# Placing attention's background steps by the vector and scalar work of each slot

## What is computed

```python
h = x @ w_in                                  # q | k | v | u, 512 columns each
z = q k^T / 8;  mask: key before query        # 8 heads of 64
log_beta = log_sigmoid(z); log_1m = where(mask, log_beta - z, 0)
after = reverse_cumsum(log_1m) - log_1m
a_out = where(mask, exp(log_beta + after), 0) @ v      # stick-breaking attention
p_out = ((trailing mean of u, windows 2,4,8,16) - u) @ pool_w * pool_scale
x1 = LayerNorm(ALPHA*x + concat[a_out, p_out] @ w_out)
y  = LayerNorm(ALPHA*x1 + (silu(x1 @ w_gate) * (x1 @ w_up)) @ w_down)
```

## Time and profile before

| | us |
|---|---|
| runs | 2577.51, 2580.75, 2580.77 (median 2580.75) |
| the profiled execution's own time | 2577.73 |
| its span (first to last instruction) | 2576.0 |
| TensorE busy | 2513.8 |
| VectorE busy | 1571.3 |
| ScalarE busy | 1153.8 |
| GpSimd busy | 1173.1 |
| granted TensorE clock, share of full speed | 0.998 |

### The profile page before, as it was taken

The page is one execution under the profiler, slowest core; times in us unless marked ns, Lnnn a source line. Parts: engine busy times, 40 slices in busy tenths (PEclk is TensorE's granted clock), DMA queues, the critical chain, the costliest instruction groups (busy, mean ns, idle before and its releaser), DMA issues.

```text
span 2576.0 us, 37571 instructions
## 1 busy us (share of the span) xinstructions
PE 2513.8 (98%) x13882; PEld 2143.7 (83%) x13882; DVE 1571.3 (61%) x2125; ACT 1153.8 (45%) x1932; POOL 1173.1 (46%) x1028
## 2 busy tenths in 40 slices
PE   9999999999999999999999999999999999999998
PEld 9978788788878878878788887878878887899997
DVE  3266247676444366787734567887775355866776
ACT  4466326664323135666532265656554213433333
POOL 4465437754323145565532174556653214354434
PEclk9999999999999999999999999999999999999999
DMA  7698946773456233444263244343533522323232
GB/s 232 201 275 258 365 159 197 236 218 116 130 155 216 82 107 112 126 123 119 80 227 131 90 115 119 103 112 110 155 91 114 203 66 92 97 91 115 94 95 84
DMA packets 210134, 374.30 MB, mean 145 GB/s; under 512 B 29760, under 2 KB 104128, under 8 KB 207904
## 3 DMA queue, kind: packets, MB, share of 16 engines
q1 hardware_dynamic: 209952, 371.89, 45.8%
HBM read 303.73 MB, written 68.09 MB: 144 GB/s over the span
## 4 chain that ended last, share of the span: by engine, by line
PE 81%; DVE 6%; issue 3%; POOL 3%; DMA 3%; ACT 2%; SPq 1%; DVEq 0%; POOLq 0%; ACTq 0%
PE bank L1315 26%; PE bank L1377 19%; PE bank L1265 8%; PE bank L1219 7%; PE bank L1323 7%; PE bank L1116 5%; PE bank L1164 4%; PE bank L1132 4%; DMA gw_lo_raw<-in_w_in_dram 1%; DVE left L1947 1%; POOL gw_lo L2617 1%; DVE acc L1985 1%; PE bank L1242 1%; POOL later_lad L2643 1%; DVE stats L1967 0%
## 5 line engine op out<-in xcount | busy, mean ns | idle before, releaser
L1315 PE MATMUL bank<-x1T,gw_hi 128*128 128x512 f32 (+1 forms) x2336 | 712.9, 389 | 3.7 <-DVE hT_lo_raw L2061 2.3
L2547 POOL TENSOR_TENSOR beta<-beta,left 128x512 f32<-128x512 f32 (+2 forms) x326 | 353.0, 1083 | 348.0 <-DVE left L1947 347.4
L1315 PEld LDWEIGHTS bank<-x1T,gw_hi 128*128 128x128 f32 x2336 | 419.0, 189 | 83.7 <-issue 3.2
L1315 PE MATMUL bank<-x1T,gw_lo 128*128 128x512 f32 (+1 forms) x1168 | 448.1, 384 | 0.0
L2574 POOL TENSOR_TENSOR gw_lo<-gw_lo_raw,gw_hi 128x1024 fp32r<-128x1024 f32 x70 | 181.8, 2597 | 423.1 <-ACT gw_hi L1569 422.9
L1492 ACT ACTIVATE aT<-bank 128x512 fp32r<-128x512 f32 (+2 forms) x326 | 173.6, 533 | 426.1 <-PE bank L1132 377.0
L1265 PE MATMUL bank<-x1T,gw_hi 128*128 128x256 f32 (+2 forms) x1472 | 353.4, 332 | 3.2 <-POOL gw_lo L2617 1.3
L2242 DVE TENSOR_TENSOR acc<-bank,acc 128x512 f32<-128x512 f32 x312 | 213.4, 686 | 211.0 <-PE bank L1377 207.6
L1932 DVE TENSOR_TENSOR aT<-bank,aT 128x512 fp32r<-128x512 f32 (+2 forms) x326 | 197.0, 604 | 195.1 <-ACT aT L1492 193.7
L1377 PE MATMUL bank<-dw_hi,hT_hi 128*128 128x512 f32 x728 | 295.2, 405 | 9.8 <-issue 5.8
L1377 PE MATMUL bank<-dw_lo,hT_hi 128*128 128x512 f32 x728 | 286.6, 394 | 0.0
(11 more groups left out here) (223 smaller groups left out, 4697.8 us busy)
## 6 DMA issues: line engine op xcount, KB each, us to landing
gw_lo_raw<-in_w_gate_dram SPq DMA_DIRECT2D x88, 512.0 KB, 3.6
gw_lo_raw<-in_w_up_dram SPq DMA_DIRECT2D x88, 512.0 KB, 3.7
dw_lo_raw<-in_w_down_dram SPq DMA_DIRECT2D x86, 512.0 KB, 4.4
gw_lo_raw<-in_w_in_dram SPq DMA_DIRECT2D x64, 512.0 KB, 4.4
k_st<-kT_scratch SPq DMA_DIRECT2D x160, 128.0 KB, 4.1
v_st<-v_scratch SPq DMA_DIRECT2D x80, 256.0 KB, 4.3
q_st<-qT_scratch SPq DMA_DIRECT2D x128, 128.0 KB, 4.0
wo_raw<-in_w_out_dram SPq DMA_DIRECT2D x16, 1024.0 KB, 5.6
```

Source lines behind the costliest of these rows:

```text
L1315: m = pe.matmul(gu_bank(g, n)[:, 0:w], gw[L % 4][a][:, k, :], x1T[x][:, k, first:first + w], start=k == 0 and s == 0, stop=k == KD - 1 and ...
L2547: pool.tensor_tensor(x[:, 0:w], x[:, 0:w], left[n % RL][:, 1:w + 1], ALU.mult).then_inc(a_done, 1)
```

## The change

A new function `level` moves attention's steps after `spread` has placed them. `slots_work` holds for every slot an amount of foreground work of VectorE and of ScalarE, and `step_work` gives what one step adds to each, and to TensorE. `level` walks through the slots with a backlog for both engines that shrinks by 2 a slot (and by the step's own TensorE amount), and places the next step in the first slot, at most EARLY = 3 before its even one, where the backlog is not over a limit; if a step came LATE = 5 or more after its even slot, the limit is raised by 0.1 and the block is done again. At most one step stands in a slot, as before. The steps of the other 32 tokens are not moved by the work.

Worked through by its own numbers, this moves 40 of 44 steps in block 0, 51 of 82 in block 1, 103 of 108 in block 2 and 133 of 140 in block 3; 14, 10, 76 and 104 of them by the full three slots earlier. First steps stay where they were. Neighbouring slots now hold steps more often: the longest unbroken row of steps has 12 slots in block 0 (before 4) and 8 in the others (before 3, 2 and 2). Slots 512 to 519 and 776 to 783 (down products and turned tokens between two blocks) held five steps each and hold none now.

On SyncE, block 0's residual tokens are loaded at m = 12 to 15 and its norm rows at m = MIX_ADD + 2*4 = 25 (the others' stay at 13), and `load_px` stands at slots 30, 33, 36, 39. In block 0's mixing (slots 131 to 188) that puts the residual tokens at slots 150 to 155 (before 139 to 153), the norm rows at 171 (before 152) and the next tokens at 158 to 167 (before 144 to 150). Nothing else of the program changes.

```diff
--- before.py
+++ after.py
@@ -627,12 +627,121 @@
             due.setdefault(first + before * (end - first) // total, []).append(tick)
             before += w
 
+    slots_work = [[0.0, 0.0] for _ in range(FP + SLOTS * BLOCKS)]
+
+    def add_work(s, vector, scalar):
+        if s < len(slots_work):
+            slots_work[s][0] += vector
+            slots_work[s][1] += scalar
+
+    for n in range(NP):
+        b, kind, c = place(n)
+        S = done_slot(n)
+        if n % 16 == 14 and b < BLOCKS - 1:
+            add_work(S, 1.8, 0)
+        if n + 3 < NP:
+            add_work(next(s for s, x in split_at.items() if x == n + 3), 0, 1.5)
+        if kind in (KEY, QUERY):
+            add_work(S, 1, 1.7 if kind == KEY else 0.85)
+        elif kind == VALUE:
+            add_work(S, 0, 0.85)
+            add_work(S + 4, 1, 0.85)
+        else:
+            add_work(S, 0, 0.85)
+            add_work(S + c + 1, 1, 0)
+            add_work(S + 5, 2, 0.85)
+            add_work(S + 8, 1.1, 1)
+    for b in range(1, BLOCKS):
+        for s in (-4, -3, 0, 1):
+            add_work(PS * b + s, 1.8, 1.5)
+    for s in (-4, -2, 0, 2):
+        add_work(FP + s, 1.9, 1.9)
+    for b, s in KC_AT:
+        add_work(PS * b + s + 1, 1, 0.85)
+
+    at_slot = FP
+    for b in range(BLOCKS):
+        for p in range(PAIRS):
+            for group in range(4):
+                if group == 1 and p:
+                    for _ in range(2 * tiles_of(b)):
+                        add_work(at_slot, 1, 0)
+                        at_slot += 1
+                for i in range(4):
+                    if group == 0 and p:
+                        add_work(at_slot, (1, 0, 1.2, 0)[i], (0, 0.85, 0, 0)[i])
+                    add_work(at_slot, ((0, 0, 0, 2.1), (0, 1, 0, 0), (1, 2.1, 1.2, 0), (0, 1, 0, 0))[group][i],
+                             ((0, 0, 1.5, 0), (0.85, 0, 1.5, 0), (1.5, 0.85, 0, 1.5), (0.85, 1.5, 0, 1.5))[group][i])
+                    if b and (p, group, i) in ((0, 0, 1), (0, 0, 2), (0, 0, 3), (1, 0, 0)):
+                        add_work(at_slot, 2.2, 0)
+                    if b and (p, group, i) in ((1, 1, 1), (1, 1, 2), (1, 1, 3), (2, 0, 0)):
+                        add_work(at_slot, 2.5, 0)
+                    at_slot += 1
+        if b < BLOCKS - 1:
+            for d in range(2 * BT):
+                add_work(at_slot, 1 + 1.9 * (d % 2 == 0) + 2.2 * (d == 0), 1.9 * (d % 2 == 0) + 0.85 * (d == 0))
+                at_slot += 1
+
+    def step_work(g, s):
+
+        lo, hi = SEGMENTS[g]
+        scan, turned, out = lo + s - AT_LEFT, lo + s - AT_HI, lo + s - AT_V
+        vector = scalar = tensor = 0.0
+        if lo <= lo + s < hi:
+            scalar += 1.6 * ITEMS[lo + s].width / BW
+            tensor += ITEMS[lo + s].width / BW * (0.68 if not ITEMS[lo + s].sample else 2)
+        if lo <= scan < hi:
+            vector += 1.9 * ITEMS[scan].width / BW
+        if lo <= turned < hi:
+            w = (columns(turned).stop - columns(turned).start) / BW
+            vector += w
+            scalar += 0.8 * w
+            tensor += 0.65 * w
+        if lo <= out < hi:
+            tensor += 0.68 if not ITEMS[out].sample else 2
+            if closes_group(out):
+                vector += 2.7
+                scalar += 1.7
+        return vector, scalar, tensor
+
+    EARLY, LATE = 3, 5
+
+    def level(ticks, first, end):
+
+        even = {tick: s for s in sorted(due) for tick in due[s]}
+        at = [even[tick] for tick in ticks]
+        free = [g == SAMPLE_BLOCK and s >= SAMPLE_AT - 2 for _, g, s in ticks]
+
+        def attempt(limit):
+            placed, back = [], [0.0, 0.0]
+            for s in range(first - 8, end):
+                back = [max(0.0, x + y - 2) for x, y in zip(back, slots_work[s])]
+                j = len(placed)
+                if j == len(ticks) or s < max(first, at[j] - (0 if free[j] else EARLY)):
+                    continue
+                if not free[j] and max(back) > limit:
+                    if s >= at[j] + LATE:
+                        return None
+                    continue
+                *work, tensor = step_work(*ticks[j][1:])
+                back = [max(0.0, x + y - tensor) for x, y in zip(back, work)]
+                placed.append(s)
+            return placed if len(placed) == len(ticks) else None
+
+        limit = 0.0
+        while attempt(limit) is None:
+            limit += 0.1
+        for tick, s, old in zip(ticks, attempt(limit), at):
+            due[old].remove(tick)
+            due.setdefault(s, []).append(tick)
+
     A_FROM = [72, 188, 456, 721]
     M_FROM = [128, 372, 637, 956]
     M_END = [188, 456, 721, 1022]
     NORM_FROM, NORM_EVERY = [196, 460, 725, 1022], [8, 6, 6, 3]
     for b in range(BLOCKS):
         spread([(ATTENTION, b, s) for s in range(A_STEPS[b])], A_FROM[b], M_FROM[b])
+        level([(ATTENTION, b, s) for s in range(A_STEPS[b])], A_FROM[b], M_FROM[b])
         spread([(MIX, b, s) for s in range(norm_step(b))], M_FROM[b] + 3, M_END[b])
         for x, s in enumerate(range(norm_step(b), M_STEPS[b])):
             due.setdefault(NORM_FROM[b] + NORM_EVERY[b] * x, []).append((MIX, b, s))
@@ -837,8 +946,8 @@
 
             def mixing(b, m):
                 nt = tiles_of(b)
-                t = (m - 5) // 3 if b == 0 else m - 11
-                if 0 <= t < BT and (b or m % 3 == 2):
+                t = m - 12 if b == 0 else m - 11
+                if 0 <= t < BT:
                     if b == 0:
                         sp.wait_ge(x_lo, x_before(3))
                     load_x(b, t)
@@ -846,7 +955,7 @@
                     groups = max(it.group for it in ITEMS if it.block == b) + 1
                     for u in range(2):
                         sp.wait_ge(o_stored[u], 32 * ((groups + 1 - u) // 2))
-                if m == LEAD:
+                if m == (LEAD if b else MIX_ADD + 2 * nt):
                     load_parameters(1, b)
                 if m < OVER:
                     for x in range(m * PIECES // OVER, (m + 1) * PIECES // OVER):
@@ -1015,8 +1124,8 @@
                     S = PS * b + s
                     for n in load_at.get(S, ()):
                         load_w(n)
-                    if b < BLOCKS - 1 and s in (16, 18, 20, 22):
-                        load_px(b + 1, (s - 16) // 2)
+                    if b < BLOCKS - 1 and s in (30, 33, 36, 39):
+                        load_px(b + 1, (s - 30) // 3)
                     if b == BLOCKS - 1 and s == 57:
                         load_gate(0)
                     if b == BLOCKS - 1 and s == 63:
```

## The result

**2594.44 us** median (five runs, 2590.29 to 2597.69) against 2580.75: ratio 1.0053, 95% interval 1.0042 to 1.0064. That is slower, and outside the range of 2556 to 2580; the forecast was 2567. The profiled execution has a span of 2594.1 us (before 2576.0).

What follows compares the result with a forecast made beforehand. TensorE, busy 98%, was taken as the bound. Terms of -22, +8.6, +3.2, +1.5 and -3.5 summed to -12.2 us, 2565.5 from the profiled 2577.73, raised to 2567 for that execution's low place among the runs; range 2556 to 2580.

Steps and rivals of the forecast that it cites:

- What bounds the kernel: Whole kernel: TensorE is busy 98%, so only the 62 us when it isn't busy can be won.
- Waits taken away: Attention's stretches: TensorE's short waits for a late VectorE go as the queue ahead of steps shrinks; 22 us off.
- The lower bound of 11: Least gain allowed for the waits taken away: 11 us off, if half of them have another cause.
- Third steps in a row: Blocks 1 to 3: scores 0.40 us late in every second of 43 third neighbouring steps with full scans; 8.6 us added.
- The limits' backlog: Blocks 2 and 3, catching up after slots 519 and 783: two waits of 0.8 us in each; 3.2 us added.
- Queries: Block 0's attention: denser rows leave a head's query loads little or no slack; 1.5 us added (0 to 6).
- Transfers: Block 0's mixing: loads moved out of the stretch with full DMA engines shorten TensorE's waits; 3.5 us off.
- The DMA share at 290 to 298 us: Block 0's mixing: sign of being right, the share falls under 1, from 1.04.
- The third steps' rival: Third steps pay in full and half of the waits come back: 2574 to 2580 us; chance 0.20.
- the late engine: GpSimd, uncounted by the placing, falls behind in rows of five or more steps: 18 us more, 2584; chance 0.13.
- VectorE held by GpSimd: The shared SBUF port pair: GpSimd's instructions shut out VectorE's two-input ones, keeping its queue long: 2574 to 2580 us; chance 0.05.

Runs made afterwards that it cites:

- e12: Changed kernel with slots 512 to 519 and 776 to 783 left out of the work sum, and no third neighbouring step in blocks 2 and 3: 2578.34 us, 0.9989.
- e2: Kernel before with only the change's moved transfers (SyncE edits), without the new placing of steps: 2574.21 us, 0.9970.
- e6: Changed kernel with the new placing in blocks 0 and 1 only: 2575.05 us, 0.9974.
- e11: Kernel before with the moved transfers, no `level`, and the even stretch of steps in blocks 2 and 3 ending three slots early: 2568.58 us, 0.9951.
- e10: Changed kernel with the norm's slots 512 to 519 and 776 to 783 left out of the work sum, so steps stay there: 2593.76 us, 1.0048.
- e3: Changed kernel with a third step behind two neighbouring ones forbidden in blocks 1 to 3: 2591.13 us, 1.0040.
- e13: Kernel before with only residual tokens and norm parameters moved in the mixings; the next block's tokens stay at slots 16 to 22: 2579.36 us, 0.9996.
- e14: The changed kernel run once more, unaltered, against the kernel before: 2589.85 us, 1.0042.

## Why the prediction was wrong, by its steps

**What bounds the kernel: right.** TensorE is busy for 97%, and what is won or lost is its waits and, as told below, its clock.

**Waits taken away, -22: this step failed.** In blocks 2 and 3 e12 has the new placing without its rows and without the slots kept free, and is 4 us slower than e2 (against the earlier trace rows its stretch of block 2 is 5.0 us longer, that of block 3 1.4 shorter); in blocks 0 and 1 e6 has it whole and equals e2. The term is 0 to +4 us. The prediction took from the earlier trace rows that TensorE waits for VectorE and from the earlier trace rows that VectorE isn't short of time, and concluded that its queue at a step is what the table evens out. e11 contradicts that last part: the longest queue, the shortest time. In the rows shown here the waits come from one instruction that is late for its own reason (the loop of a step, a norm, a stretched split), and such a one doesn't become earlier if a sum over slots gets lower; a step moved away from it meets another. That most of the waits are so was not counted through. The lower bound of 11, "half of the waits have another cause", was too high by 11; the trace of before couldn't have borne a bound above zero, since no row showed one wait go when its queue got shorter.

**Third steps in a row, +8.6: mechanism and price right, too few counted.** 0.18 to 0.22 us each by e10 against e12, where 0.40 / 2 = 0.20 was written. In blocks 2 and 3 the change has 46 of them (the prediction counted the 29 with a full scan), 8 to 10 us, and its statement that a delay isn't added up is shown in the one row and refuted in the other: "every second pays" holds unless VectorE has a third operation in the slot. Block 1's 28 cost nothing that e6 can show; why they don't is open, and so the price is one of blocks 2 and 3, not of every row.

**The limits' backlog, +3.2: held in size, by difference only.** The change is 11.5 to 16 us slower than e12 (2589.85 and 2594.44 less 2578.34); less 8 to 10 for its rows, 1.5 to 8 are left for the slots kept free and the catching up. e3 says 2: it has those slots nearly free (3 steps) and no such rows, and is 12.8 us slower than e12, 10.9 of it in block 1.

**Queries, +1.5: small, as said.** One wait of 1.0 us for `q_st`, in the first execution's trace, at 211.72 us, not between 150 and 205.

**Transfers, -3.5: too small alone.** The mixing's three waits went, leaving 0.2 us (a new one of 0.6 to 1.0 for an accumulator came in three traces), and its slots take 3.4 to 4.6 us less in every trace with all loads moved. By the times the transfers alone win 7.5. The DMA share at 290 to 298 us didn't fall below 1, as had been written. The changed kernel is 7 us behind there; where about the same slots stand, at 297 to 305 us, it is 0.91, but in e2, which wins the time all the same, 1.02 (at 293 to 301 us). So the share doesn't tell the gain. Both stretches of the changed kernel, columns as above:

```profile
290.00:298.00 8.00, 7.84 (x36) 6.10 (x35) 2.85 (x4) 4.96 (x5) 3.32 (x2) 1.00 1.02 357
297.00:305.00 8.00, 8.00 (x52) 7.20 (x51) 5.51 (x3) 3.80 (x4) 7.82 (x3) 1.00 0.91 326
```

Between 1.0049 for the placing and 0.9970 for the transfers one would expect 1.002 for both, or 2586; measured were 1.0053 and 1.0042. That gap of 4 to 8 us is open: no trace shows the transfers' gain undone, except the first one's loss in block 0's projection. By e13, moving `load_px` is most of the gain. Its traces put 3 us of that in block 0's mixing, which the prediction had counted; that `load_px` of the other blocks costs nothing, as it says, is neither shown nor refuted.

Part of these differences goes with the granted clock. Its mean over a kernel's executions is 0.9966 for before (63 executions beside the runs), 0.9954 and 0.9968 for the change and e14, 0.9977 for e2, 0.9980 for e11, 0.9953 for e12 and 0.9946 for e3. Among the 63 executions of before, 0.001 less clock goes with some 1.5 us more time. By that estimate the clock has some 2 of e11's 12 us, 1.6 of e2's 7.5, 3.5 of the 4 us between e12 and e2, and 1 to 3 us of the gap. In the traces the clock falls to 0.50 for 3.4 or 6.8 us at a time, twice in block 2's stretch of e12 and never in that of e2 or before. Whether the placing brings such falls on wasn't tested.

**The rivals.** The third steps' rival had the right mechanism with -16 for the waits taken away, where 0 was right. GpSimd did not become the late engine: TensorE's waits for its product, which the prediction named as a sign of being wrong, are 2.0 us in 3 places (before 0.8 in one; e12 3.7 in 4). The sum with the measured terms: 0 to +4, +11.5 to +16 for rows and backlog together, +1, less 4 to 7.5, is +5 to +17 us; measured +9 to +14.

## What to carry to other kernels

A table that evens out the sum of an engine's work evens out something that nobody may be waiting for: before pricing such a change at the waits it is to remove, take one wait and follow what it waited for. Where a step closes a loop over several engines that is longer than the slot (3.59 us against 3.19), an empty slot behind each pair is worth more than a short queue. A planner that searches for the least limit needs a second aim below it; with "earliest slot under the limit" one crowded place sets the pace for a whole block.

## What the runs showed of the hardware

**VectorE held by GpSimd.** The prediction gave this rival 0.05 and read it off one long split. It is regular: of the 86 subtractions `hT_lo`, 0.68 us in the middle, 12 take over a microsecond in the trace of before and 13 in that of the change, and each of the 25 ends 0.55 us (one 0.54) after an instruction of GpSimd ends. One that a matmul then waits for, in the changed kernel:

```profile
952.06 2.40 POOL L2683 TENSOR_TENSOR gw_lo<-gw_lo_raw,gw_hi 128x1024 fp32r<-128x1024 f32 x1
...
952.75 2.25 DVE L2337 TENSOR_TENSOR hT_lo<-hT_lo_raw,hT_hi 128x512 fp32r<-128x512 f32 x1 [0.70 <-ACT hT_hi L1777]
...
955.62 0.41 PE L1241 MATMUL bank<-begin,beta 128*128 128x128 f32 x2 [1.60 <-DVE aT L2041]
```

and in e10 behind two of GpSimd's in a row:

```profile
945.18 2.40 POOL L2682 TENSOR_TENSOR gw_lo<-gw_lo_raw,gw_hi 128x1024 fp32r<-128x1024 f32 x1
...
945.87 4.56 DVE L2336 TENSOR_TENSOR hT_lo<-hT_lo_raw,hT_hi 128x512 fp32r<-128x512 f32 x1 [0.70 <-ACT hT_hi L1776]
...
947.53 2.35 POOL L2663 TENSOR_TENSOR acc<-acc,bias 128x1024 f32<-128x1024 f32 x1
...
951.05 0.66 PE L1240 MATMUL bank<-begin,beta 128*128 128x128 f32 x2 [3.92 <-DVE aT L2040]
```

945.87 + 4.56 = 950.43, and 947.53 + 2.35 + 0.55 = 950.43. The subtraction of 0.68 us didn't get in between the two: the one that waited was passed over for a second instruction. It cost TensorE 3.92 us, the longest wait for VectorE in any of these traces. The Trainium skill, SBUF — State Buffer, section "SBUF: two separate sides", says that such a pair excludes each other for whole instructions, and these rows agree. VectorE's instructions take 66 us more than their medians in the changed kernel (63 in e14) and 56, 59, 57 and 51 in before, e2, e12 and e11, so the placing does move this too; how much of the time that is wasn't taken apart.

**A late weight and the clock.** In the first execution of the change a weight landed late beside the next block's tokens, and TensorE's clock went down behind the wait. ScalarE's and TensorE's rows, and the stretch after:

```profile
80.17 1.06 ACT L1790 ACTIVATE gw_hi<-gw_lo_raw 128x1024 fp32r<-128x1024 f32 x1 [5.83 <-DMA gw_lo_raw<-in_w_in_dram]
```

```profile
87.89 1.65 PE L1404 MATMUL bank<-first_d,pw 128*128 128x512 f32 x3 [2.37 <-DVE first_d L2416]
```

```profile
87.60:94.40 6.80, 6.51 (x27) 6.22 (x28) 1.15 (x3) 2.79 (x6) 4.75 (x2) 0.50 0.59 198
```

The granted clock is 0.50 (1.2 of 2.4 GHz) for 6.8 us, and TensorE does 27 matmuls in that time; before, 45 in 6.0 us at 1.00. By slot 72 the trace is 3.7 us behind that of before. e2's trace has the like (2.6 us behind, the clock down for 3.4 us); the ten others with these loads have at most 0.6 by slot 48, the second one of the change among them.
